# Activation tiles stored in pairs with 16 free bytes behind each pair

## The chip, the cores and the metric

The kernel runs on one core of a Trainium2 chip. The metric is the time on the device in microseconds (us); the kernel before takes 2249.84 us, the median of three runs (2249.45 to 2250.53).

## What is computed

Two layers of a decoder trunk on a sequence of 256 tokens, model width 2048. Cut to what matters:

```
for l in range(2):
    h = rms_norm(x, pre_mix_norm[l])
    p = h @ w_in[l]                      # 2048 x 5648: q, k, v, z, xBC, dt
    A = causal attention (8 heads x 128, rotary on 32 dims)
    S = Mamba-2 scan (16 heads x 64, 2 groups, state 128, chunks of 128)
    y = concat(rms_norm(A), group_rms_norm(S * silu(z))) @ w_out[l]     # 2048 x 2048
    x = x + rms_norm(y, post_mix_norm[l])
    u = square(relu(rms_norm(x, pre_mlp_norm[l]) @ w_up[l]))            # 2048 x 8192
    x = x + rms_norm(u @ w_down[l], post_mlp_norm[l])                   # 8192 x 2048
```

All inputs and outputs are float32.

## The kernel before

**Split products.** The large products are done in fp32r, TensorE's fast float32 form. To keep accuracy each operand is split in a high part and a rest: a product a * w becomes a_hi * w_hi + a_lo * w_hi + a_hi * w_lo, three matmuls. The order of these differs by line, their number doesn't.

**The weights' ring.** Weights come in chunks of 256 rows by 512 columns (NC = 8 chunks make a block of 2048 rows by 512 columns). SyncE's queue loads chunk c into raw[c % 4] (L296), ScalarE copies it to w_hi[c % 4] in fp32r (round_hi, L462), VectorE subtracts to get w_lo[c % 4] (split_lo, L1028), and TensorE then uses the chunk. ScalarE writes a slot once TensorE is done with it, SyncE's next load waits for split_lo. The ring has four slots, and the splitting runs three chunks ahead.

**The activations.** a_hi and a_lo hold the normed x, transposed: 16 tiles (k) of 128 partitions (features) by 256 tokens. u_hi and u_lo hold, at different times, the mixer's output and a quarter of the MLP's inner activations in the same form. Chunk c needs tiles 2c and 2c + 1, a pair. They are written by ScalarE (x_hi, L494; to_hi, L518; the square in up_pair, L646) and VectorE (x_lo, L1074; to_lo, L1089; L1375). In the mixer the first two pairs of u are also scratch of the scan, seg_hi and seg_lo, written by GpSimd (L416) and read by L825 and L826.

**Feature chunks and token chunks.** feature_chunk (L706) has the weights' tile as TensorE's stationary operand (128 x 128) and streams 256 columns of a: 24 matmuls of 256 columns per chunk (L734, 736, 737; for the first chunk after a norm L720, 722, 727). token_chunk (L690) has it the other way round: a 128 x 128 piece of a or u is stationary and 512 columns of w_hi or w_lo are streamed: 12 matmuls of 512 columns per chunk (L699 to 701). Feature chunks serve 7 of the 15 blocks of the mixer and the 16 blocks of w_up, token chunks the 8 other blocks of the mixer (v, z, w_out) and the 16 blocks of w_down, in each layer. inv_row_and_dt (L755) multiplies wdt_both, weights that lie outside the ring, with all 16 tiles of a (L769, 770).

**Order.** TensorE's program is written out by hand: block after block, chunk after chunk, with the small matmuls of attention and scan put in after chosen chunks. The MLP's four quarters run in a hardware loop, so that u's tiles are addressed there by a register (bass.ds).

**Where things lie.** Each tensor is a stretch of bytes in every partition; they lie one behind another in the order of their declaration (raw, w_hi, w_lo, x_sb, a_hi, a_lo, u_hi, u_lo, ybuf, xbcT, x_tok, v_tok, zg, b_tok, convr, wk, cbm, wdt_both, ident, ...), each rounded up to 32 bytes. raw to u_lo take 16,384 bytes each. A tile of a or u is 1024 bytes, a ring slot 4096.

Of the kernel before, what the change touches and what calls it, by code (L numbers as in the profile page):

```python
# [50 lines left out]
CK = 2  # L51
CB = 512
NC = KT // CK
W = CK * CB
WARM = 12
AHEAD = 3
# [70 lines left out]
def trunk(nc, x, positions, pre_mix_norm, post_mix_norm, pre_mlp_norm, post_mlp_norm, w_in, conv_w,  # L127
          conv_b, dt_bias, a_log, d_skip, attn_out_norm, ssd_out_norm, w_out, w_up, w_down, out):
    ctx = ExitStack()
    with ctx:  # L130
# [5 lines left out]
        w_hi = sb("w_hi", [P, RING, W], F32R)  # L136
        w_lo = sb("w_lo", [P, RING, W], F32R)
        x_sb = sb("x_sb", [P, TT, D])
        a_hi = sb("a_hi", [P, KT, SEQ], F32R)
        a_lo = sb("a_lo", [P, KT, SEQ], F32R)  # L140
        u_hi = sb("u_hi", [P, KT, SEQ], F32R)
        u_lo = sb("u_lo", [P, KT, SEQ], F32R)
        ybuf = sb("ybuf", [P, TT * D])
        xbcT = sb("xbcT", [P, NCT, SEQ])
        x_tok = sb("x_tok", [P, TT, SW])
# [50 lines left out]
        tab = x_tok[0:ROPE, :, :].rearrange("p t n -> p (t n)")  # L196
        tab_f, tab_m = tab[:, 0:HALF], tab[:, HALF:ROPE]
        tab_pos, tab_angle, tab_turn, tab_sin = (tab[:, i * SEQ:(i + 1) * SEQ] for i in range(1, 5))
        seg_hi = [u_hi[:, 2 * i:2 * i + 2].rearrange("p k s -> p (k s)") for i in range(2)]
        seg_lo = [u_lo[:, 2 * i:2 * i + 2].rearrange("p k s -> p (k s)") for i in range(2)]  # L200
        seg_e = wk[:, 1]
        tab_first, tab_last = x_tok[0:ROPE, 1, 2 * CB - 4:2 * CB], x_tok[0:ROPE, 1, 2 * CB - 8:2 * CB - 4]
        low_w, cmask_w, wdt_w = v_tok[:, 0, 0:P], v_tok[:, 0, P:2 * P], v_tok[:, 0, 2 * P:3 * P - 2 * SH]
# [243 lines left out]
        def _(act):  # L447
# [27 lines left out]
            with act.Fori(0, DEPTH) as l:  # L475
# [13 lines left out]
                def x_hi(n, j, gain):  # L489

                    act.wait_ge(*upto("xT_mm", l, 8 * n + j + 1))
                    for kk in range(2):
                        k = 2 * j + kk
                        ins = act.activation(a_hi[:, k], M[j % 4][:, kk * SEQ:(kk + 1) * SEQ], ACT.Copy,  # L494
                                             scale=prm[:, gain + k:gain + k + 1])
                    ins.then_inc(sem["xT_hi"], 1)

# [15 lines left out]
                def to_hi(name, n, j, bank, gain):  # L513

                    act.wait_ge(*upto(name + "_mm", l, n))
                    for kk in range(2):
                        k = 2 * j + kk
                        ins = act.activation(u_hi[:, k], M[bank][:, kk * SEQ:(kk + 1) * SEQ], ACT.Copy,  # L518
                                             scale=prm[:, gain + k:gain + k + 1])
                    ins.then_inc(sem[name + "_hi"], 1)  # L520

# [99 lines left out]
                def up_pair(q, i):  # L621

                    for j in range(2):
                        b = l * NB + q * (2 * QB) + i * 2 + (B_MLP + j)
                        first = j == 0 and is_first(q, i)
                        for c in range(AHEAD, NC + AHEAD):
                            split = (lambda: round_hi(b, c)) if c < NC else (lambda: round_hi(b + 1, c - NC))
                            if first:
                                norm_turn(1, c, G_MLP, split)
                            else:  # L630
                                split()
                        if first:
# [45 lines left out]
        def _(pe):  # L678
# [11 lines left out]
            def token_chunk(c, par, s_hi, s_lo, tile_first=False):  # L690


                for i in range(CK * TT):
                    kk, t = (i % CK, i // CK) if tile_first else (i // TT, i % TT)
                    k = c * CK + kk
                    wh, wl = (w[:, c % RING, kk * CB:(kk + 1) * CB] for w in (w_hi, w_lo))
                    o = acc[par][t][:]
                    sh, sl = (s[:, k, t * P:(t + 1) * P] for s in (s_hi, s_lo))
                    pe.matmul(o, sh, wh, start=(k == 0), stop=False)  # L699
                    pe.matmul(o, sh, wl, start=False, stop=False)  # L700
                    ins = pe.matmul(o, sl, wh, start=False, stop=(k == KT - 1))  # L701
                    if tile_first and i == CK - 1:
                        ins.then_inc(sem["tile_done"], 1)
                ins.then_inc(sem["mm_done"], 1)

            def feature_chunk(c, par, lo_ready=None):  # L706
# [8 lines left out]
                if lo_ready:  # L715

                    for kk in range(CK):
                        k = c * CK + kk
                        for m in range(CB // P):
                            pe.matmul(o(m), w(w_hi, kk, m), a_hi[:, k], start=(k == 0 and m % 2 == 0), stop=False,  # L720
                                      skip_group_check=True)
                            pe.matmul(o(m), w(w_lo, kk, m), a_hi[:, k], start=False, stop=False,
                                      skip_group_check=True)
                    pe.wait_ge(*lo_ready)
                    for kk in range(CK):
                        for m in range(CB // P):
                            ins = pe.matmul(o(m), w(w_hi, kk, m), a_lo[:, c * CK + kk], start=False, stop=False,
                                            skip_group_check=True)
                    ins.then_inc(sem["mm_done"], 1)
                    return  # L730
                for kk in range(CK):
                    k = c * CK + kk
                    for m in range(CB // P):
                        pe.matmul(o(m), w(w_hi, kk, m), a_hi[:, k], start=(k == 0 and m % 2 == 0), stop=False,  # L734
                                  skip_group_check=True)
                        pe.matmul(o(m), w(w_hi, kk, m), a_lo[:, k], start=False, stop=False, skip_group_check=True)  # L736
                        ins = pe.matmul(o(m), w(w_lo, kk, m), a_hi[:, k], start=False, stop=(k == KT - 1),  # L737
                                        skip_group_check=True)
                ins.then_inc(sem["mm_done"], 1)

            with pe.Fori(0, DEPTH) as l:
# [13 lines left out]
                def inv_row_and_dt():  # L755
# [259 lines left out]
        def _(dve):  # L1015
# [45 lines left out]
            with dve.Fori(0, DEPTH) as l:  # L1061
# [8 lines left out]
                def x_lo(n, j, gain):  # L1070
                    dve.wait_ge(*upto("xT_hi", l, 8 * n + j + 1))
                    for kk in range(2):
                        k = 2 * j + kk
                        ins = dve.scalar_tensor_tensor(a_lo[:, k], M[j % 4][:, kk * SEQ:(kk + 1) * SEQ],  # L1074
                                                       prm[:, gain + k:gain + k + 1], a_hi[:, k].bitcast(F32),
                                                       ALU.mult, ALU.subtract)
                    ins.then_inc(sem["xT_ready"], 1)

# [6 lines left out]
                def to_lo(name, n, j, bank, gain):  # L1085
                    dve.wait_ge(*upto(name + "_hi", l, n))
                    for kk in range(2):
                        k = 2 * j + kk
                        ins = dve.scalar_tensor_tensor(u_lo[:, k], M[bank][:, kk * SEQ:(kk + 1) * SEQ],  # L1089
                                                       prm[:, gain + k:gain + k + 1], u_hi[:, k].bitcast(F32),  # L1090
                                                       ALU.mult, ALU.subtract)
                    ins.then_inc(sem[name + "_ready"], 1)

# [248 lines left out]
                def up_pair(q, i):  # L1342
                    for j in range(2):
# [21 lines left out]
                        for k in range(2):  # L1365
# [9 lines left out]
                            dve.tensor_tensor(ul.rearrange("p k s -> p (k s)"), wk[:, 2 + k],  # L1375
                                              uh.rearrange("p k s -> p (k s)").bitcast(F32),
                                              ALU.subtract).then_inc(sem["u_ready"], 1)

                def down_pair(q, i):
                    for j in range(2):  # L1380
# [62 lines left out]
```

## Time and profile before

| | |
|---|---|
| median of three runs | 2249.84 us |
| span of the profiled execution (first to last instruction) | 2248.1 us |
| PE (TensorE matmuls) busy | 2216.5 us, 99% |
| DVE (VectorE) busy | 1319.9 us, 59% |
| ACT (ScalarE) busy | 1016.3 us, 45% |
| POOL (GpSimd) busy | 109.9 us, 5% |
| mean granted TensorE clock | 0.998 of full |
| HBM | 402.58 MB read, 180 GB/s over the span |

The profiled execution's own time is its span, 2248.1 us, 1.7 us under the median of the runs. Matmuls are pipelined: the record of one begins when it begins and ends when its last result is modelled to be out, while the next has long begun. So the busy time of PE counts overlapping records once, and the mean length of one says less than the distance from one start to the next, which the timeline gives.

### The profile page before, as it was taken

To read this page: it belongs to the slowest core of one execution; us is meant where nothing else is said; L and a number is where in the kernel's file an instruction comes from. 1 tells how busy PE (TensorE), PEld (TensorE's weight loads), DVE (VectorE), ACT (ScalarE), POOL (GpSimd) and SP (SyncE) were. 2 spreads that over 40 slices of the span, in tenths; PEclk is the share of its full clock that TensorE was granted. 3 is DMA by queue.
4 is the path that set the end of the run, shared out by engine and by line. 5 is a ranking of instruction groups with operands and counts; after the bars stand their busy time and mean duration, and the time that the engine had idled before them with its cause. 6 is when DMAs were issued, how large, how long until landed. Compare 5 with 4: busy or idle time off the path is not lost.

```text
span 2248.1 us, 39497 instructions
## 1 busy us (share of the span) xinstructions
PE 2216.5 (99%) x14282; PEld 2023.7 (90%) x14282; DVE 1319.9 (59%) x1528; ACT 1016.3 (45%) x1280; POOL 109.9 (5%) x112
## 2 busy tenths in 40 slices
PE   8999999999999999999999999999999999999997
PEld 8999888998998998898899988889989989988986
DVE  6777465655555455555578775657554545554555
ACT  5443464543444344344454435545434434443443
POOL 2141000000000000000001410000000000000000
PEclk9999999999999999999999999999999999999999
DMA  6555556556656656655645555655666566556565
GB/s 204 152 170 157 161 188 198 177 179 200 189 180 192 190 179 193 190 184 187 193 125 166 166 161 151 198 185 182 190 192 186 173 201 188 184 189 193 176 194 163
DMA packets 208448, 406.21 MB, mean 181 GB/s; under 512 B 12540, under 2 KB 12820, under 8 KB 207828
## 3 DMA queue, kind: packets, MB, share of 16 engines
q1 hardware_dynamic: 206660, 398.04, 57.3%
q10 hardware_dynamic: 992, 4.78, 0.6%
q0 software_dynamic: 688, 1.90, 0.4%
q8 instruction: 72, 1.18, 0.2%
q14 instruction: 36, 0.29, 0.0%
HBM read 402.58 MB, written 2.10 MB: 180 GB/s over the span
## 4 chain that ended last, share of the span: by engine, by line
issue 71%; PE 26%; DVE 1%; ACT 0%; POOL 0%; DMA 0%; DVEq 0%; POOLq 0%; ACTq 0%
PE acc L734 5%; PE acc L737 5%; PE acc L736 5%; PE acc L699 3%; PE acc L701 3%; PE acc L700 3%; PE M L838 1%; PE M L751 1%; DVE x_sb L1111 0%; PE M L859 0%; DVE xbcT L1177 0%; DMA wk<-in_ssd_out_norm 0%; PE M L879 0%; POOL st L393 0%; DVE w_lo L1028 0%
## 5 line engine op out<-in xcount | busy, mean ns | idle before, releaser
L1028 DVE TENSOR_TENSOR w_lo<-raw,w_hi 128x1024 fp32r<-128x1024 f32 x755 | 927.7, 1235 | 793.4 <-ACT w_hi L462 790.1
L462 ACT ACTIVATE w_hi<-raw 128x1024 fp32r<-128x1024 f32 x755 | 794.5, 1058 | 1026.8 <-PE acc L701 521.6
L734 PE MATMUL acc<-a_hi,w_hi 128*128 128x256 f32 x2912 | 828.4, 284 | 1.8 <-DVE w_lo L1028 1.8
L736 PE MATMUL acc<-a_lo,w_hi 128*128 128x256 f32 x2912 | 823.9, 283 | 0.0
L737 PE MATMUL acc<-a_hi,w_lo 128*128 128x256 f32 x2912 | 823.9, 283 | 0.0
L734 PEld LDWEIGHTS acc<-a_hi,w_hi 128*128 128x128 f32 x2912 | 558.6, 192 | 4.1 <-DVE w_lo L1028 2.7
L736 PEld LDWEIGHTS acc<-a_lo,w_hi 128*128 128x128 f32 x2912 | 558.7, 192 | 1.8 <-issue 1.0
L737 PEld LDWEIGHTS acc<-a_hi,w_lo 128*128 128x128 f32 x2912 | 558.7, 192 | 0.0
L699 PE MATMUL acc<-w_hi,u_hi 128*128 128x512 f32 x1280 | 498.6, 390 | 0.0
L700 PE MATMUL acc<-w_lo,u_hi 128*128 128x512 f32 x1280 | 498.0, 389 | 0.0
L701 PE MATMUL acc<-w_hi,u_lo 128*128 128x512 f32 x1280 | 498.0, 389 | 0.0
L701 PEld LDWEIGHTS acc<-w_hi,u_lo 128*128 128x128 f32 x1280 | 240.3, 188 | 50.0
L699 PEld LDWEIGHTS acc<-w_hi,u_hi 128*128 128x128 f32 x1280 | 240.3, 188 | 49.4
L700 PEld LDWEIGHTS acc<-w_lo,u_hi 128*128 128x128 f32 x1280 | 240.3, 188 | 49.4
L699 PE MATMUL acc<-w_hi,a_hi 128*128 128x512 f32 x256 | 102.6, 401 | 0.0
L701 PE MATMUL acc<-w_hi,a_lo 128*128 128x512 f32 x256 | 100.0, 391 | 0.0
L700 PE MATMUL acc<-w_lo,a_hi 128*128 128x512 f32 x256 | 99.8, 390 | 0.0
L393 POOL TENSOR_TENSOR st<-st,minus_half 128x2 f32<-128x2 f32 x12 | 9.1, 757 | 1786.3 <-DVE st L1100 1403.0
L1368 DVE TENSOR_TENSOR wk<-wk 128x512 f32<-128x512 f32 x64 | 44.0, 688 | 39.1 <-ACT wk L642 39.1
L642 ACT ACTIVATE wk<-acc 128x512 f32<-128x512 f32 x64 | 37.7, 589 | 62.2 <-PE acc L737 62.2
L701 PEld LDWEIGHTS acc<-w_hi,a_lo 128*128 128x128 f32 x256 | 48.0, 188 | 10.3
L700 PEld LDWEIGHTS acc<-w_lo,a_hi 128*128 128x128 f32 x256 | 48.2, 188 | 9.0
(218 smaller groups left out, 1049.2 us busy)
## 6 DMA issues: line engine op xcount, KB each, us to landing
raw<-in_w_up SPq DMA_DIRECT2D x256, 512.0 KB, 3.7
raw<-in_w_down SPq DMA_DIRECT2D x256, 512.0 KB, 4.5
raw<-in_w_in SPq DMA_DIRECT2D x179, 512.0 KB, 3.8
raw<-in_w_out SPq DMA_DIRECT2D x64, 512.0 KB, 4.6
zg<-in_post_mix_norm ACTq DMA_DIRECT2D x2, 1024.0 KB, 4.6
zg<-in_post_mlp_norm ACTq DMA_DIRECT2D x2, 1024.0 KB, 6.4
out<-x_sb SPq DMA_DIRECT2D x8, 256.0 KB, 2.8
x_sb<-in_x POOLq DMA_DIRECT2D x3, 512.0 KB, 7.3
```

The costliest lines, as they stand in the source:

```text
L462: act.activation(w_hi[:, c % RING], raw[:, c % RING], ACT.Copy).then_inc(sem["hi_ready"], 1)
L642: act.activation(wk[:, k], acc[1 - j][k][:], ACT.Relu).then_inc(acc_free[1 - j], 1)
L699: pe.matmul(o, sh, wh, start=(k == 0), stop=False)
L700: pe.matmul(o, sh, wl, start=False, stop=False)
L701: ins = pe.matmul(o, sl, wh, start=False, stop=(k == KT - 1))
L734: pe.matmul(o(m), w(w_hi, kk, m), a_hi[:, k], start=(k == 0 and m % 2 == 0), stop=False, skip_group_check=True)
L736: pe.matmul(o(m), w(w_hi, kk, m), a_lo[:, k], start=False, stop=False, skip_group_check=True)
L737: ins = pe.matmul(o(m), w(w_lo, kk, m), a_hi[:, k], start=False, stop=(k == KT - 1), skip_group_check=True)
L751: ins = pe.transpose(M[j % 4][:, kk * SEQ + t * P:kk * SEQ + (t + 1) * P], x_sb[:, t, k * P:(k + 1) * P], ident[:])
L838: ins = pe.matmul(M[3 * g][:, o:o + SP_], seg_e[:, h * P:(h + 1) * P], x_tok[:, t, g * CB + o:g * CB + o + SP_], start=True, stop=True)
L1028: dve.tensor_tensor(w_lo[:, c % RING], raw[:, c % RING], w_hi[:, c % RING].bitcast(F32), ALU.subtract).then_inc(sem["split_done"], 1)
L1368: dve.tensor_tensor(wk[:, 2 + k], wk[:, k], wk[:, k], ALU.mult)\
```

## The change

The four activation tensors get the shape [128, 8, 2 * 256 + 4] in place of [128, 16, 256]: each pair of tiles (2 KB) is followed by four float32 values, 16 bytes, that nothing writes or reads. A helper tile(a, k) gives tile k. All users of a_hi, a_lo, u_hi and u_lo address through it or through the pair; nothing else is changed.

```diff
+STEP = 4
-        a_hi = sb("a_hi", [P, KT, SEQ], F32R)
+        a_hi = sb("a_hi", [P, NC, CK * SEQ + STEP], F32R)
...
-        u_lo = sb("u_lo", [P, KT, SEQ], F32R)
+        u_lo = sb("u_lo", [P, NC, CK * SEQ + STEP], F32R)
...
-        seg_hi = [u_hi[:, 2 * i:2 * i + 2].rearrange("p k s -> p (k s)") for i in range(2)]
+        seg_hi = [u_hi[:, i, 0:2 * SEQ] for i in range(2)]
...
+        def tile(a, k):
+
+            return a[:, k // CK, k % CK * SEQ:(k % CK + 1) * SEQ]
...
-                            u = u_hi[:, 8 * i + 4 * j + 2 * k:8 * i + 4 * j + 2 * k + 2] if type(i) is int else \
-                                u_hi[:, bass.ds(i * 8 + (4 * j + 2 * k), 2)]
-                            act.activation(u.rearrange("p k s -> p (k s)"), wk[:, k], ACT.Square)\
+                            u = u_hi[:, 4 * i + 2 * j + k, 0:2 * SEQ] if type(i) is int else \
+                                u_hi[:, bass.ds(i * 4 + (2 * j + k), 1), 0:2 * SEQ].rearrange("p a n -> p (a n)")
+                            act.activation(u, wk[:, k], ACT.Square)\
...
-                    sh, sl = (s[:, k, t * P:(t + 1) * P] for s in (s_hi, s_lo))
+                    sh, sl = (tile(s, k)[:, t * P:(t + 1) * P] for s in (s_hi, s_lo))
...
-                        pe.matmul(o(m), w(w_hi, kk, m), a_lo[:, k], start=False, stop=False, skip_group_check=True)
-                        ins = pe.matmul(o(m), w(w_lo, kk, m), a_hi[:, k], start=False, stop=(k == KT - 1),
+                        pe.matmul(o(m), w(w_hi, kk, m), tile(a_lo, k), start=False, stop=False, skip_group_check=True)
+                        ins = pe.matmul(o(m), w(w_lo, kk, m), tile(a_hi, k), start=False, stop=(k == KT - 1),
...
-                        pe.matmul(o, w, a_hi[:, k], start=(k == 0), stop=False)
-                        ins = pe.matmul(o, w, a_lo[:, k], start=False, stop=(k == KT - 1))
+                        pe.matmul(o, w, tile(a_hi, k), start=(k == 0), stop=False)
+                        ins = pe.matmul(o, w, tile(a_lo, k), start=False, stop=(k == KT - 1))
...
-                            k0 = i * 8 + (4 * j + 2 * k)
-                            uh, ul = (a[:, k0:k0 + 2] if type(i) is int else a[:, bass.ds(k0, 2)]
+                            k0 = i * 4 + (2 * j + k)
+                            uh, ul = (a[:, k0, 0:2 * SEQ] if type(i) is int else
+                                      a[:, bass.ds(k0, 1), 0:2 * SEQ].rearrange("p a n -> p (a n)")
```

x_hi, to_hi, x_lo, to_lo and the first chunk's matmuls (L720, 722, 727) change in the same way, a[:, k] to tile(a, k).

## Rows read from the trace of the kernel before

**Rows 1.** The page: span, and PE's busy time, its share and instructions.
```profile
span 2248.1 us, 39497 instructions
...
PE 2216.5 (99%) x14282; PEld 2023.7 (90%) x14282; DVE 1319.9 (59%) x1528; ACT 1016.3 (45%) x1280; POOL 109.9 (5%) x112
```

**Rows 2.** The page: the chain that ended last, by engine.
```profile
issue 71%; PE 26%; DVE 1%; ACT 0%; POOL 0%; DMA 0%; DVEq 0%; POOLq 0%; ACTq 0%
```

**Rows 3.** Waits of PE: line, waited for: us in total, times, longest.
```profile
PE M L683 <- DMA wk<-in_ssd_out_norm: 8.7, 1, 8.7
```

**Rows 4.** Groups by line, PE: out<-in, shapes, count | busy us, mean ns.
```profile
L734 PE MATMUL acc<-a_hi,w_hi 128*128 128x256 f32 x2912 | 828.4, 284 | 1.8 <-DVE w_lo L1028 1.8
...
L699 PE MATMUL acc<-w_hi,u_hi 128*128 128x512 f32 x1280 | 498.6, 390 | 0.0
...
L699 PE MATMUL acc<-w_hi,a_hi 128*128 128x512 f32 x256 | 102.6, 401 | 0.0
```

**Rows 5.** Timeline, feature chunk, first and last of 18: start us, length us, instruction.
```profile
799.90 0.28 PE L734 MATMUL acc<-a_hi,w_hi 128*128 128x256 f32 x1
...
801.94 0.28 PE L737 MATMUL acc<-a_hi,w_lo 128*128 128x256 f32 x1
```

**Rows 6.** Timeline, token chunks, first and last of 22.
```profile
900.02 0.39 PE L701 MATMUL acc<-w_hi,u_lo 128*128 128x512 f32 x1
...
904.78 0.39 PE L701 MATMUL acc<-w_hi,u_lo 128*128 128x512 f32 x1
```

**Rows 7.** Timeline, dt projection: of 5 early ones, then of 25 later ones.
```profile
41.64 0.28 PE L770 MATMUL M<-a_lo,wdt_both 128*128 128x256 f32 x1
...
42.12 0.28 PE L770 MATMUL M<-a_lo,wdt_both 128*128 128x256 f32 x1
...
42.34 0.28 PE L770 MATMUL M<-a_lo,wdt_both 128*128 128x256 f32 x1
...
45.06 0.28 PE L770 MATMUL M<-a_lo,wdt_both 128*128 128x256 f32 x1
```

**Rows 8.** Timeline, fp32 matmuls: ident with itself; probabilities with values, six pairs.
```profile
396.68 2.84 PE L926 MATMUL M<-ident 128*128 128x128 f32 x24
...
1399.67 0.38 PE L892 MATMUL M<-v_tok,wk 128*128 128x128 f32 x2
...
1400.79 0.39 PE L895 MATMUL M<-v_tok,wk 128*128 128x128 f32 x2
```

**Rows 9.** Timeline, token chunk just after small matmuls, first and last of 5.
```profile
1391.73 0.40 PE L700 MATMUL acc<-w_lo,a_hi 128*128 128x512 f32 x1
...
1392.65 0.39 PE L701 MATMUL acc<-w_hi,a_lo 128*128 128x512 f32 x1
```

**Rows 10.** Groups by line, DVE and ACT: the writes of u.
```profile
L1375 DVE TENSOR_TENSOR u_lo<-wk,u_hi 128x512 f32 (+1 forms) x64 | 44.3, 692 | 13.7 <-ACT u_hi L646 7.0 <-DVE wk L1368 5.7
...
L646 ACT ACTIVATE u_hi<-wk 128x512 f32 (+1 forms) x64 | 40.5, 633 | 7.1
```

**Rows 11.** Waits of ACT for PE.
```profile
ACT w_hi L462 <- PE acc L701: 521.6, 332, 2.3
ACT w_hi L462 <- PE acc L737: 496.9, 280, 5.2
```

**Rows 12.** Timeline, DVE and ACT beside a feature chunk.
```profile
801.91 1.22 DVE L1028 TENSOR_TENSOR w_lo<-raw,w_hi 128x1024 fp32r<-128x1024 f32 x1 [1.66 <-ACT w_hi L462]
803.70 1.06 ACT L462 ACTIVATE w_hi<-raw 128x1024 fp32r<-128x1024 f32 x1 [1.82 <-PE acc L737]
```

**Rows 13.** Windows, mixer and MLP of layer 1: busy us by engine, PEclk, DMA share, GB/s.
```profile
26.00:412.00 386.00, 382.59 (x2472) 346.84 (x2471) 259.17 (x351) 182.08 (x266) 47.98 (x34) 1.00 0.55 166
412.00:1134.00 722.00, 718.49 (x4620) 657.63 (x4619) 391.48 (x388) 316.50 (x357) 2.71 (x4) 1.00 0.60 187
```

**Rows 14.** The page: loads of w_down, count, KB, us from issue to landing.
```profile
raw<-in_w_down SPq DMA_DIRECT2D x256, 512.0 KB, 4.5
```

More of the change, by code:

```diff
@@ L138, in trunk @@
         x_sb = sb("x_sb", [P, TT, D])
-        a_hi = sb("a_hi", [P, KT, SEQ], F32R)
-        a_lo = sb("a_lo", [P, KT, SEQ], F32R)
-        u_hi = sb("u_hi", [P, KT, SEQ], F32R)
-        u_lo = sb("u_lo", [P, KT, SEQ], F32R)
+        a_hi = sb("a_hi", [P, NC, CK * SEQ + STEP], F32R)
+        a_lo = sb("a_lo", [P, NC, CK * SEQ + STEP], F32R)
+        u_hi = sb("u_hi", [P, NC, CK * SEQ + STEP], F32R)
+        u_lo = sb("u_lo", [P, NC, CK * SEQ + STEP], F32R)
         ybuf = sb("ybuf", [P, TT * D])
@@ L198, in trunk @@
         tab_pos, tab_angle, tab_turn, tab_sin = (tab[:, i * SEQ:(i + 1) * SEQ] for i in range(1, 5))
-        seg_hi = [u_hi[:, 2 * i:2 * i + 2].rearrange("p k s -> p (k s)") for i in range(2)]
-        seg_lo = [u_lo[:, 2 * i:2 * i + 2].rearrange("p k s -> p (k s)") for i in range(2)]
+        seg_hi = [u_hi[:, i, 0:2 * SEQ] for i in range(2)]
+        seg_lo = [u_lo[:, i, 0:2 * SEQ] for i in range(2)]
         seg_e = wk[:, 1]
@@ L493, in x_hi @@
                         k = 2 * j + kk
-                        ins = act.activation(a_hi[:, k], M[j % 4][:, kk * SEQ:(kk + 1) * SEQ], ACT.Copy,
+                        ins = act.activation(tile(a_hi, k), M[j % 4][:, kk * SEQ:(kk + 1) * SEQ], ACT.Copy,
                                              scale=prm[:, gain + k:gain + k + 1])
@@ L517, in to_hi @@
                         k = 2 * j + kk
-                        ins = act.activation(u_hi[:, k], M[bank][:, kk * SEQ:(kk + 1) * SEQ], ACT.Copy,
+                        ins = act.activation(tile(u_hi, k), M[bank][:, kk * SEQ:(kk + 1) * SEQ], ACT.Copy,
                                              scale=prm[:, gain + k:gain + k + 1])
@@ L719, in feature_chunk @@
                         for m in range(CB // P):
-                            pe.matmul(o(m), w(w_hi, kk, m), a_hi[:, k], start=(k == 0 and m % 2 == 0), stop=False,
+                            pe.matmul(o(m), w(w_hi, kk, m), tile(a_hi, k), start=(k == 0 and m % 2 == 0), stop=False,
                                       skip_group_check=True)
-                            pe.matmul(o(m), w(w_lo, kk, m), a_hi[:, k], start=False, stop=False,
+                            pe.matmul(o(m), w(w_lo, kk, m), tile(a_hi, k), start=False, stop=False,
                                       skip_group_check=True)
@@ L726, in feature_chunk @@
                         for m in range(CB // P):
-                            ins = pe.matmul(o(m), w(w_hi, kk, m), a_lo[:, c * CK + kk], start=False, stop=False,
+                            ins = pe.matmul(o(m), w(w_hi, kk, m), tile(a_lo, c * CK + kk), start=False, stop=False,
                                             skip_group_check=True)
@@ L733, in feature_chunk @@
                     for m in range(CB // P):
-                        pe.matmul(o(m), w(w_hi, kk, m), a_hi[:, k], start=(k == 0 and m % 2 == 0), stop=False,
+                        pe.matmul(o(m), w(w_hi, kk, m), tile(a_hi, k), start=(k == 0 and m % 2 == 0), stop=False,
                                   skip_group_check=True)
-                        pe.matmul(o(m), w(w_hi, kk, m), a_lo[:, k], start=False, stop=False, skip_group_check=True)
-                        ins = pe.matmul(o(m), w(w_lo, kk, m), a_hi[:, k], start=False, stop=(k == KT - 1),
+                        pe.matmul(o(m), w(w_hi, kk, m), tile(a_lo, k), start=False, stop=False, skip_group_check=True)
+                        ins = pe.matmul(o(m), w(w_lo, kk, m), tile(a_hi, k), start=False, stop=(k == KT - 1),
                                         skip_group_check=True)
@@ L1073, in x_lo @@
                         k = 2 * j + kk
-                        ins = dve.scalar_tensor_tensor(a_lo[:, k], M[j % 4][:, kk * SEQ:(kk + 1) * SEQ],
-                                                       prm[:, gain + k:gain + k + 1], a_hi[:, k].bitcast(F32),
+                        ins = dve.scalar_tensor_tensor(tile(a_lo, k), M[j % 4][:, kk * SEQ:(kk + 1) * SEQ],
+                                                       prm[:, gain + k:gain + k + 1], tile(a_hi, k).bitcast(F32),
                                                        ALU.mult, ALU.subtract)
@@ L1088, in to_lo @@
                         k = 2 * j + kk
-                        ins = dve.scalar_tensor_tensor(u_lo[:, k], M[bank][:, kk * SEQ:(kk + 1) * SEQ],
-                                                       prm[:, gain + k:gain + k + 1], u_hi[:, k].bitcast(F32),
+                        ins = dve.scalar_tensor_tensor(tile(u_lo, k), M[bank][:, kk * SEQ:(kk + 1) * SEQ],
+                                                       prm[:, gain + k:gain + k + 1], tile(u_hi, k).bitcast(F32),
                                                        ALU.mult, ALU.subtract)
@@ L1371, in up_pair @@
                             dve.wait_ge(*upto("u_hi_ready", l, n + 1))
-                            k0 = i * 8 + (4 * j + 2 * k)
-                            uh, ul = (a[:, k0:k0 + 2] if type(i) is int else a[:, bass.ds(k0, 2)]
+                            k0 = i * 4 + (2 * j + k)
+                            uh, ul = (a[:, k0, 0:2 * SEQ] if type(i) is int else
+                                      a[:, bass.ds(k0, 1), 0:2 * SEQ].rearrange("p a n -> p (a n)")
                                       for a in (u_hi, u_lo))
-                            dve.tensor_tensor(ul.rearrange("p k s -> p (k s)"), wk[:, 2 + k],
-                                              uh.rearrange("p k s -> p (k s)").bitcast(F32),
-                                              ALU.subtract).then_inc(sem["u_ready"], 1)
+                            dve.tensor_tensor(ul, wk[:, 2 + k], uh.bitcast(F32), ALU.subtract)\
+                                .then_inc(sem["u_ready"], 1)
                 def down_pair(q, i):
```

## The prediction

> **What bounds the kernel now.** I read the engine shares first: PE is busy for 2216.5 of 2248.1 us [rows 1]. "Busy" overlaps here, so I then read the chain of waits: 71% of the span is "issue", time in which the instruction at the end of the chain waited for nothing that the profile shows, and 26% is PE itself [rows 2]. PE's longest wait for another engine is 8.7 us, once, before the first matmul [rows 3]. So the end is set by how closely one matmul follows another. The groups by line show what these matmuls are [rows 4]: feature matmuls with 256 moving columns (L734, 736, 737, 2912 of each) and token matmuls with 512 (L699 to 701, 1536 of each over the two kinds of input, of which the rows show 1280 and 256). With the 96 of L720, 722 and 727 that makes 8832 + 4608 = 13,440 split-precision matmuls. The 283 and 390 ns in these rows are the time of one from start to modelled end; what counts is from start to start. In the timeline 17 feature steps take 801.94 - 799.90 = 2.04 us, 120.0 ns each [rows 5]; 21 token steps take 904.78 - 900.02 = 4.76 us, 226.7 ns each [rows 6]. 8832 x 120.0 + 4608 x 226.7 ns = 1060 + 1045 = 2105 us of the span of 2248.1: nothing else is large.
>
> At the granted full clock (2.4 GHz, PEclk 1.00 in the windows [rows 13]) 256 columns are 106.7 ns and 512 are 213.3 ns. Each matmul thus costs 13.3 ns more than its columns, the same for both lengths. It is a price for each matmul and its weight load, not for each column. That price is what the change can touch.
>
> **Is the price tied to addresses?** Tensors lie one behind another in the order in which they are declared. In w_hi, w_lo, a_hi, a_lo, u_hi and u_lo every tile that a main matmul reads starts at a multiple of 512 bytes from the others, so the weights being loaded and the operand being streamed always stand at distance 0 modulo 128 bytes. One group of the same form doesn't: the dt projection (L769, 770) takes its weights from wdt_both, behind convr, whose 4144 bytes are rounded up to 4160, so they stand 64 bytes off modulo 128. Its 256-column matmuls begin at the usual pace (41.64 to 42.12 us, four steps, 120 ns), and then settle: 24 steps take 45.06 - 42.34 = 2.72 us, 113.3 ns each [rows 7]. The difference of 6.67 ns is 16 columns at 2.4 GHz, and 13.3 ns is twice that. 120.0, 226.7 and 113.3 ns are 18, 34 and 17 such steps: the pace looks quantized, and an operand's place seems to decide whether one quantum is lost or two. Against it: fp32 matmuls don't care. With ident as both operands (distance 0) 24 take 2.84 us, (2.84 - 0.275) / 23 = 111.5 ns; with wk and v_tok, 64 bytes apart modulo 128, 10 steps take 1400.79 - 1399.67 = 1.12 us, 112 ns [rows 8]. Those stream each column in two passes, so they are weaker evidence than the dt group, but dt also differs from the rest by lying far away in SBUF.
>
> A rule of the Trainium skill speaks against the change here. The page "SBUF — State Buffer", section "Who interferes with whom", gives PE separate read ports for the moving operand and for the weights, and says that PE and ACT never wait on anyone; by it the sum would be zero. The traces agree only for the fp32 rows; the 6.67 ns of the dt rows has no place in it. The page "TensorE: Matmul & The Clock Gate", section "Back-to-back issue gap", would put a warm matmul of 256 columns at 109.2 ns; that this kernel's stands at 120.0 is a price that the page doesn't have.
>
> **The change part by part.** (1) Pair p of a and u starts at p x 2064 bytes instead of p x 2048, and each of the four tensors grows by 128 bytes. Modulo 128 the tensors' bases, and all that is behind them, stay where they were, and pair p is 16p bytes off: 0, 16, ..., 112. Chunk c of every block reads pair c with ring slot c % 4, so one eighth of all main matmuls (1680) meets each distance. Chunk 0 is unchanged. (2) One quantum saved in an eighth is 1680 x 6.67 ns = 11.2 us, feature and token alike, since the price is per matmul (that it also holds for token matmuls, where u or a is the weight, is not shown by any row). (3) How many of the seven shifted eighths gain? The trace shows distance 64 alone (pair 4). Ends: one eighth, 11.2 us; all seven, 78.4 us. Below nothing: a distance could also lose a quantum; seven that lose one are +78.4 us. The nearest row for a slower pace is the token matmuls after a pause, 1392.65 - 1391.73 = 0.92 us for four, 230 ns [rows 9], only half a quantum. I take four eighths, as if the loss faded evenly from distance 0 to 64 and back (weights 0, 1/4, 1/2, 3/4, 1, 3/4, 1/2, 1/4 sum to 4): 4 x 11.2 = 44.8 us. (4) The dt matmuls are 64, and pairs 0 and 4 change roles there: below 0.5 us. The segment-sum weights on POOL and L825, 826 keep pairs 0 and 1: 32 matmuls, nothing.
>
> (5) The instructions keep their number and shapes: tile() gives the same 256 contiguous values, the u writes remain 512 contiguous values, and the register index is i * 4 instead of i * 8. ACT and DVE write 64 such tiles each, 633 and 692 ns a piece [rows 10]; were they a tenth slower it would be 4.0 and 4.4 us of their time, hidden because ACT waits 1018.5 us for PE in all [rows 11]. With that cover gone it would cost those 4 us. The weights' DMAs don't change.
>
> (6) What is late next, once PE is faster? A chunk of 24 feature matmuls takes 2.88 us; ACT and DVE spend 1.06 and 1.22 us on it [rows 12], and both finish long before the slot is used again. DVE is busy for 259 of 386 us in the mixer and 391 of 722 in the MLP [rows 13]. A raw slot is freed at 801.91 + 1.22 = 803.13 us and wanted by ACT at 803.70 - 2.88 + 4 x 2.88 = 812.3 us: 9.2 us for a load that lands in 4.5 us [rows 14]. The DMA rate rises from 187 to about 191 GB/s at a share of 0.60. So I let nothing come back.
>
> Sum: against the profiled execution's 2248.1 us, 2248.1 - 44.8 = 2203.3 us. The median of the runs is 1.7 us above that span: 2205.0 us.
>
> **Rivals.** No change: the 13.3 ns are PE's own price for a fp32r weight swap whatever the address, and dt is faster for another reason (its weights' region, or always writing one place in PSUM). For: the pace is 120 for every m, k and ring slot, and the fp32 rows. Against: within the feature matmuls, too, the written half bank stays for three matmuls and none of these is at 113. Time 2249.8 us. Slower: at some distances the weight load runs just behind the stream over the same lines and catches it more often, a third quantum. It decides as soon as more eighths lose than gain; with five up and two down it is net three, +33.6 us, 2283 us. For: distance 0 may be a favourable meeting, as the ident rows, at 111.5 ns the fastest non-transposing ones here, have it; against: dt at 64 is faster, and no steady pace in this trace is above 226.7 or 120.0. Gain eaten: PE speeds up but the mixer, where DVE is busiest, makes PE wait for split chunks; half is given back, 2227 us; the slack in (6) speaks against it.
>
> **How the numbers follow.** PE's pace improves for one to seven eighths: 0.48, with its own range 2171 (2249.8 - 78.4) to 2239 (2249.8 - 11.2). No change: 0.29. Slower: 0.18. Gain eaten: 0.05, also faster. Differences below 0.2% (4.5 us) can't be told from none here. Faster is 0.48 + 0.05 = 0.53, same 0.29, slower 0.18. The range holds the first two cases and the fourth, and some of the third: 2170 to 2258; the rest of slower, about 0.15, is left out.
>
> **What would show it.** In the changed kernel the start-to-start time, chunk by chunk, is the whole test: chunk 0 still at 120.0 and 226.7 ns, chunk 4 at 113.3 and 220.0, the other six at one or the other. The dt group should invert: pair 4 at 120. PE's other waits stay within a few us, and ACT's wait for PE shrinks by about the gain. If all eight chunks stay at 120.0 the address idea is wrong; if chunk 4 alone gains, the time is 2239; if token chunks don't follow feature chunks, step (2) is wrong, and the eighths are worth 7.4 us each.

## The result and the profile after

The changed kernel is slower: 2258.98 us (median of 5 runs, 2258.76 to 2259.58) against 2249.82 us for the kernel before (5 runs, 2249.32 to 2250.53). The ratio is 1.0042, with a 95% interval of 1.003 to 1.0055: small, but clear of the noise.

The page of the changed kernel, span and busy times, answers to [rows 1]:

```profile
span 2257.7 us, 39497 instructions
...
PE 2226.5 (99%) x14282; PEld 2010.4 (89%) x14282; DVE 1319.0 (58%) x1528; ACT 1016.8 (45%) x1280; POOL 111.7 (5%) x112
...
issue 71%; PE 26%; DVE 1%; ACT 0%; POOL 0%; DMA 0%; DVEq 0%; POOLq 0%; ACTq 0%
```

Instructions, chain and the busy times of the other engines are those of before; PE alone has 10.0 us more. Its waits for others hardly grew (for w_lo from 1.8 to 2.2 us in all); the first row answers to [rows 3] (8.7 us):

```profile
PE M L688 <- DMA wk<-in_ssd_out_norm: 8.6, 1, 8.6
PE M L756 <- DVE x_sb L1116: 4.1, 3, 2.2
```

So the matmuls themselves came at another pace. The groups by line show that it went both ways. They answer to [rows 4], where L734 (now L739) had 284 ns, L699 (now L704) 390 ns with u and 401 with a:

```profile
L739 PE MATMUL acc<-a_hi,w_hi 128*128 128x256 f32 x2912 | 820.0, 282 | 2.2 <-DVE w_lo L1033 2.2
L742 PE MATMUL acc<-a_hi,w_lo 128*128 128x256 f32 x2912 | 818.6, 281 | 0.0
L741 PE MATMUL acc<-a_lo,w_hi 128*128 128x256 f32 x2912 | 815.7, 280 | 0.0
...
L704 PE MATMUL acc<-w_hi,u_hi 128*128 128x512 f32 x1280 | 506.6, 396 | 0.0
...
L704 PE MATMUL acc<-w_hi,a_hi 128*128 128x512 f32 x256 | 103.8, 405 | 0.0
```

Feature matmuls became shorter by 1 to 3 ns, token matmuls longer by 4 to 6. The timeline gives the pace. First a block of feature chunks: the first matmul of its chunk 0 and of its chunk 7, 168 steps later.

```profile
811.74 0.28 PE L739 MATMUL acc<-a_hi,w_hi 128*128 128x256 f32 x1
...
831.55 0.28 PE L739 MATMUL acc<-a_hi,w_hi 128*128 128x256 f32 x1
```

19.81 / 168 = 117.9 ns, where [rows 5] had 120.0. Then a block of token chunks, 84 steps:

```profile
677.11 0.40 PE L704 MATMUL acc<-w_hi,u_hi 128*128 128x512 f32 x1
...
696.59 0.39 PE L704 MATMUL acc<-w_hi,u_hi 128*128 128x512 f32 x1
```

19.48 / 84 = 231.9 ns, where [rows 6] had 226.7. Nor is the pace even any more. These are seven steps within a chunk 4:

```profile
823.06 0.28 PE L739 MATMUL acc<-a_hi,w_hi 128*128 128x256 f32 x1
823.17 0.28 PE L741 MATMUL acc<-a_lo,w_hi 128*128 128x256 f32 x1
823.29 0.28 PE L742 MATMUL acc<-a_hi,w_lo 128*128 128x256 f32 x1
823.41 0.28 PE L739 MATMUL acc<-a_hi,w_hi 128*128 128x256 f32 x1
...
823.76 0.28 PE L739 MATMUL acc<-a_hi,w_hi 128*128 128x256 f32 x1
823.88 0.28 PE L741 MATMUL acc<-a_lo,w_hi 128*128 128x256 f32 x1
```

Every three matmuls (w_hi with a_hi, w_hi with a_lo, w_lo with a_hi) take 0.35 us, but the single steps repeat as about 118, 114 and 122 ns. Before, all were 120.

From here on "pace" is the mean distance from one start to the next over all matmuls of a kind in a trace, steps over 140 ns (feature) and 245 ns (token) left out, which are pauses.

| | feature | token on a | token on u |
|---|---|---|---|
| matmuls | 8832 | 768 | 3840 |
| before, ns | 119.93 | 227.95 | 226.76 |
| changed, ns | 118.00 | 232.03 | 232.70 |
| difference x count, us | -17.0 | +3.1 | +22.8 |

The sum is +8.9 us, and 9.2 us were measured: all but 0.3 us of the result is the pace of PE.

By chunk, with the hi parts at 0, 16, ..., 112 bytes from the ring and the lo parts 128 bytes further, the changed kernel's feature pace is 117.87, 117.92, 117.79, 117.65, 117.72, 118.19, 118.17, 118.65 ns. The token pace (u, w_down) is 232.5, 234.9, 232.5, 231.3, 231.6, 232.6, 233.0, 232.9. Chunk 0, which I held to be unchanged, is as different as the rest, and no chunk stands at 113.3. The dt group, of which I had said that pair 4 would go to 120, slowed as a whole: its last 24 steps take 118.2 ns on average, where they took 113.3.

### The profile page after: what moved, and what is told of

Its sections match the earlier page's. It is cut to its first block, busy times and chain, and to the rows that moved or that the text cites. A ratio compares the mean times of both kernels' runs of the same rounds, so it can differ in the third digit from the quotient of the medians.

```text
span 2257.7 us, 39497 instructions
## 1 busy us (share of the span) xinstructions
PE 2226.5 (99%) x14282; PEld 2010.4 (89%) x14282; DVE 1319.0 (58%) x1528; ACT 1016.8 (45%) x1280; POOL 111.7 (5%) x112
## 4 chain that ended last, share of the span: by engine, by line
issue 71%; PE 26%; DVE 1%; ACT 0%; POOL 0%; DMA 0%; DVEq 0%; POOLq 0%; ACTq 0%
PE acc L739 5%; PE acc L742 5%; PE acc L741 4%; PE acc L704 3%; PE acc L706 3%; PE acc L705 3%; PE M L843 1%; PE M L756 1%; PE M L864 0%; DVE xbcT L1182 0%; DVE x_sb L1116 0%; DMA wk<-in_ssd_out_norm 0%; PE acc L725 0%; PE M L884 0%; POOL st L398 0%
## 5 line engine op out<-in xcount | busy, mean ns | idle before, releaser
L739 PE MATMUL acc<-a_hi,w_hi 128*128 128x256 f32 x2912 | 820.0, 282 | 2.2 <-DVE w_lo L1033 2.2
L741 PE MATMUL acc<-a_lo,w_hi 128*128 128x256 f32 x2912 | 815.7, 280 | 0.0
L739 PEld LDWEIGHTS acc<-a_hi,w_hi 128*128 128x128 f32 x2912 | 549.2, 189 | 4.6 <-DVE w_lo L1033 3.1
L741 PEld LDWEIGHTS acc<-a_lo,w_hi 128*128 128x128 f32 x2912 | 547.2, 188 | 1.9 <-issue 1.0
L742 PEld LDWEIGHTS acc<-a_hi,w_lo 128*128 128x128 f32 x2912 | 547.9, 188 | 0.0
L704 PE MATMUL acc<-w_hi,u_hi 128*128 128x512 f32 x1280 | 506.6, 396 | 0.0
L705 PE MATMUL acc<-w_lo,u_hi 128*128 128x512 f32 x1280 | 505.1, 395 | 0.0
L706 PE MATMUL acc<-w_hi,u_lo 128*128 128x512 f32 x1280 | 505.0, 395 | 0.0
L704 PEld LDWEIGHTS acc<-w_hi,u_hi 128*128 128x128 f32 x1280 | 240.6, 188 | 55.2
L704 PE MATMUL acc<-w_hi,a_hi 128*128 128x512 f32 x256 | 103.8, 405 | 0.0
```

Of the source, the lines that this page charges most:

```text
L739: pe.matmul(o(m), w(w_hi, kk, m), tile(a_hi, k), start=(k == 0 and m % 2 == 0), stop=False, skip_group_check=True)
L741: pe.matmul(o(m), w(w_hi, kk, m), tile(a_lo, k), start=False, stop=False, skip_group_check=True)
L742: ins = pe.matmul(o(m), w(w_lo, kk, m), tile(a_hi, k), start=False, stop=(k == KT - 1), skip_group_check=True)
```

## The experiments

The kernel before ran beside each of them, with medians of 2249.4 to 2249.6 us. The granted clock was 0.997 or 0.998 of full in all traces.

**Which part does it?** First the bases alone, 128 free bytes behind each tensor and no gaps inside:

```diff
         a_hi = sb("a_hi", [P, KT, SEQ], F32R)
+        tail0 = sb("tail0", [P, 32])
         a_lo = sb("a_lo", [P, KT, SEQ], F32R)
+        tail1 = sb("tail1", [P, 32])
...
```

> No gaps inside the tensors, but 128 free bytes behind each of a_hi, a_lo, u_hi and u_lo, so that their bases stand where the changed kernel has them. Base theory (the 128 bytes between a hi part and its lo part do it, as chunk 0 of the changed kernel, whose pair has no gap ahead of it, also left 120.0 ns): feature matmuls at about 117.9 ns, token matmuls at about 232.5 ns in every chunk, near 2259 us. Gap theory (the growing distance between ring and pair does it): 120.0 and 226.7 ns, 2250 us. The theory of the prediction, distance modulo 128: 2250 us.

Measured: 2251.13 us, ratio 1.0007 (0.9998 to 1.0017). Feature 117.79 ns, the same in all chunks; token on a 231.2, on u 231.12. One block of each, 168 feature steps and 84 token steps:

```profile
607.25 0.28 PE L738 MATMUL acc<-a_hi,w_hi 128*128 128x256 f32 x1
...
627.04 0.28 PE L738 MATMUL acc<-a_hi,w_hi 128*128 128x256 f32 x1
...
854.29 0.39 PE L703 MATMUL acc<-w_hi,u_hi 128*128 128x512 f32 x1
...
873.71 0.39 PE L703 MATMUL acc<-w_hi,u_hi 128*128 128x512 f32 x1
```

19.79 / 168 = 117.8 ns and 19.42 / 84 = 231.2 ns. Both paces moved, in opposite directions, and the shifts cancel in the total: by the total alone, nothing happened. A move by 128 bytes is not neutral, which ends the prediction's "modulo 128". The base theory was right in its direction, and about the feature pace. Its time, 2259 us, was missed by 8 us, because the token pace is 231.1 and not 232.5. So the two parts of the change divide like this: the moved bases give the whole gain of the feature matmuls and three quarters of the loss of the token matmuls, +1.7 us together, and the 16-byte gaps add the other 7.9 of the 9.2 us (1.6 ns more on each of the 3840 token matmuls that read u are 6.1 us of it).

Gaps in a alone (after's tile() kept, u without gaps and declared first):

```diff
+        u_hi = sb("u_hi", [P, NC, CK * SEQ], F32R)
+        u_lo = sb("u_lo", [P, NC, CK * SEQ], F32R)
         a_hi = sb("a_hi", [P, NC, CK * SEQ + STEP], F32R)
         a_lo = sb("a_lo", [P, NC, CK * SEQ + STEP], F32R)
-        u_hi = sb("u_hi", [P, NC, CK * SEQ + STEP], F32R)
-        u_lo = sb("u_lo", [P, NC, CK * SEQ + STEP], F32R)
```

> The 16-byte gaps in a_hi and a_lo alone; u_hi and u_lo are declared first, without gaps, at the old distances. Role theory (an operand off the ring's alignment speeds the matmuls in which it is streamed up, 119.9 to 118.0 ns, and slows those in which it is the stationary one, 227 to 232.6 ns): 8832 feature matmuls gain 17 us, the 768 token matmuls that read a lose 4 us, 2237 us. If gaps in any tensor slow the whole: over 2250 us. The prediction's theory has no loss in it, so it would want 2250 or less for this one too.

Measured: 2236.74 us, ratio 0.9943 (0.9927 to 0.996). By line, feature and token on u:

```profile
L739 PE MATMUL acc<-a_hi,w_hi 128*128 128x256 f32 x2912 | 819.8, 282 | 2.2 <-DVE w_lo L1033 2.2
...
L704 PE MATMUL acc<-w_hi,u_hi 128*128 128x512 f32 x1280 | 498.7, 390 | 0.0
```

Gaps in u alone (a_hi and a_lo without, u_hi and u_lo with them):

> The gaps in u_hi and u_lo alone. Role theory: feature matmuls stay at 119.9 ns, the 3840 token matmuls that read u lose 5.6 ns each, 2250 + 22 = 2272 us. If only gaps in the streamed operand mattered: 2250 us.

Measured: 2273.29 us, ratio 1.0105 (1.0088 to 1.0122). The same two lines:

```profile
L739 PE MATMUL acc<-a_hi,w_hi 128*128 128x256 f32 x2912 | 828.3, 284 | 1.8 <-DVE w_lo L1033 1.8
...
L704 PE MATMUL acc<-w_hi,u_hi 128*128 128x512 f32 x1280 | 506.6, 396 | 0.0
```

The two halves are separate and add up: -12.7 (a) and +23.9 (u) make +11.2 us, where both together measured 9.2. Only the matmuls that read the moved tensor change: token on u stays at 226.8 ns with gaps in a, feature at 119.9 with gaps in u. The role theory puts it so: moved a is a gain, since most matmuls on it stream it; moved u is a loss, since all matmuls on it hold it as the stationary operand while the ring is streamed. The role theory's times, 2237 and 2272 us, were met within 1.3 us.

All four tensors at a common 64 bytes, which is the dt projection's distance:

```diff
+        ahead = sb("ahead", [P, 16])
         a_hi = sb("a_hi", [P, KT, SEQ], F32R)
```

> No gaps, but 64 free bytes ahead of a_hi: all four tensors stand 64 bytes off the ring, their hi and lo parts at the old distance from each other. Distance theory of the prediction (64 bytes is the dt projection's distance, 113.3 ns): feature 113.3 and token 220.0 ns in every chunk, 13,440 x 6.67 ns less, 2160 us. If it holds for the streamed role only, and tokens lose 5.6 ns: 2250 - 59 + 26 = 2217 us. If a common distance does nothing and only unequal hi and lo parts do: 2250 us.

Measured: 2258.4 us, ratio 1.004 (1.0026 to 1.0054). Feature 117.50 ns, token 233.3 in every chunk; here 84 token steps of one block:

```profile
676.44 0.39 PE L700 MATMUL acc<-w_hi,u_hi 128*128 128x512 f32 x1
...
696.04 0.39 PE L700 MATMUL acc<-w_hi,u_hi 128*128 128x512 f32 x1
```

19.60 / 84 = 233.3 ns. A common distance with hi and lo in step changes both paces, so it is not only the distance between hi and lo that counts. But 64 bytes do not give a mean of 113.3 (2160 us; 24 of the 368 feature chunks have that pace), and the mixed forecast of 2217 us failed as well, because it took 113.3 for the feature matmuls.

**A map of distances.** Pair of hi, pair of lo and a gap in one tensor, so that hi and lo of a chunk always keep the same distance and chunk c stands at c gaps. The edit for gaps of 128 bytes (32 floats):

```diff
+        a_both = sb("a_both", [P, NC, 2 * CK * SEQ + 32], F32R)
+        a_hi, a_lo = (a_both[:, :, i * CK * SEQ:(i + 1) * CK * SEQ] for i in range(2))
```

> u_hi and u_lo at the old distances. a_hi and a_lo lie in one tensor, pair by pair (pair of hi, pair of lo, 128 free bytes), so that hi and lo of a chunk always stand at the same distance from the ring modulo 2048, and chunk c at 128c bytes: a scan of 0, 128, ..., 896 with equal parts. If only the distance between streamed parts mattered (the 128 bytes between a_hi and a_lo in the changed kernel), or if the distance counts modulo 128: feature 120.0 ns in all chunks, 2250 us. If the distance between weights and streamed operand counts in a longer period: 120.0 in chunk 0, about 117 to 118 in the others; the 768 token matmuls of a about 232 ns where a is off; some 2237 us.

> The same with 16 free bytes: chunk c at 16c bytes, hi and lo alike, a scan of 0 to 112. If any distance but 0 gives the pace of the run with all 64 off: feature 120.0 in chunk 0, about 117.5 in the seven others, 2249.4 - 7/8 x 8832 x 2.4 ns + token matmuls of a 768 x 7/8 x 6.3 ns = 2235 us. If a distance below 32 or 64 bytes still meets the same place: 120.0 in chunks 1 to 3 too, 2242 us.

> The 16-byte scan with 128 bytes ahead of it: chunk c at 128 + 16c bytes. If the period is 128 bytes: the same list as in the first scan (119.7, 118.7, 116.8, 118.3, 117.4, 119.8, 119.9, 113.8), 2237 us. If it is 256 bytes, as the 128-byte scan says (119.7 at even multiples, 118.9 at odd ones): 118.9 in chunk 0 and another list behind it; 2230 to 2245 us.

> The scan with 4 free bytes: chunk c at 4c bytes, 0 to 28. If SBUF is read in lines of 16 bytes and only the line counts: chunks 0 to 3 at one pace near 120.0 ns, chunks 4 to 7 near the 118.7 of 16 bytes. If an operand that starts within a line also costs a line more: chunks 1 to 3 and 5 to 7 slower than 0 and 4. If single bytes count: a different pace in each. Between 2235 and 2260 us.

Measured: 2246.5 us for the scan by 128 bytes (ratio 0.9987, 0.9978 to 0.9997), 2236.9 for 16 (0.9945, 0.9928 to 0.9961), 2237.94 for 16 with 128 ahead (0.9948, 0.9931 to 0.9964), and 2241.3 in one run for 4 bytes. Feature pace by chunk, ns:

| chunk | 0 | 1 | 2 | 3 | 4 | 5 | 6 | 7 |
|---|---|---|---|---|---|---|---|---|
| 128c bytes | 119.67 | 118.82 | 119.68 | 118.97 | 119.70 | 118.82 | 119.68 | 118.90 |
| 16c | 119.72 | 118.74 | 116.77 | 118.31 | 117.43 | 119.77 | 119.86 | 113.80 |
| 128 + 16c | 119.08 | 118.68 | 118.16 | 119.22 | 115.67 | 119.23 | 118.12 | 117.30 |
| 4c | 119.48 | 122.62 | 117.55 | 116.70 | 113.82 | 122.09 | 120.32 | 115.88 |

The first line alternates: the even multiples of 128 bytes are alike, and so are the odd ones, so the pattern repeats after 256 bytes. The second and third lines differ, as they may if 128 bytes are not the period. (They prove less than the first, because one distance can have more than one pace, as the last experiment shows.) The last line says that bytes count, down to 4: 122.6 at 4 bytes is the slowest pace of all, and my guess of 16-byte lines fell. All mean token paces on a in these scans are 228.4 ns or more: no distance beats 226.7.

The forecasts did less well than some of the times suggest. The 128-byte scan met neither of its two (2250 and 2237 us): the odd multiples came to 118.9 and not to 117 or 118, and the even ones stayed. The 16-byte scan's 2236.9 lies beside its 2235, but by luck: the chunks spread from 113.8 to 119.9 ns instead of standing at 117.5. The ranges for the other two held, and were wide.

**Is the dt projection fast because of its distance?**

```diff
+        pad0 = sb("pad0", [P, 16])
         w_lo = sb("w_lo", [P, RING, W], F32R)
+        pad1 = sb("pad1", [P, 240])
...
+        pad2 = sb("pad2", [P, 16])
         wdt_both = sb("wdt_both", [P, 2 * KT * SH + P - 2 * SH], F32R)
```

> a and u as in the kernel before, at distance 0 from w_hi (modulo 1024); w_lo 64 bytes further off, and wdt_both moved by 64 bytes, so that the dt projection now stands at distance 0 modulo 128. The prediction's reading of the dt rows: dt slows from 113.3 to 120.0 ns. Against it (its pace has another cause): dt stays near 113.3. For the main matmuls: w_lo is now off both as weights (feature) and as stream (token), so feature about 118 and token about 232 ns if every matmul next to an off one is touched, 2258 us; if nothing but a and u's own place matters, 2250 us.

Measured: 2254.39 us, ratio 1.0021 (1.0011 to 1.003). The last 23 matmuls of the dt projection, first and last:

```profile
42.34 0.27 PE L773 MATMUL M<-a_lo,wdt_both 128*128 128x256 f32 x1
...
44.92 0.28 PE L773 MATMUL M<-a_lo,wdt_both 128*128 128x256 f32 x1
```

2.58 / 22 = 117.3 ns against 113.3 in [rows 7]: it does depend on the addresses. It is no test of distance 0, though. With a period of 256 bytes, and since the dt weights step by 128 bytes from k to k, dt stood at 64 and 192 bytes in turn before, and stands at 0 and 128 in turn here.

Distance, or the place of one operand? The dt groups of three runs answer it. In the kernel before, a is at 0 and wdt_both at 64 or 192, modulo 256. In this run a is at 0 and wdt_both at 0 or 128. In the run with a alone at 64 bytes (below), wdt_both is at 0 or 128 as here, and a at 64. There the last 24 steps are:

```profile
41.51 0.28 PE L771 MATMUL M<-a_lo,wdt_both 128*128 128x256 f32 x1
...
44.23 0.28 PE L771 MATMUL M<-a_lo,wdt_both 128*128 128x256 f32 x1
```

2.72 / 24 = 113.3 ns, the pace of before. Both operands stand elsewhere than before, at the same distance, and the pace is the same; the weights stand as in this run, at another distance, and the pace is another. So it is the distance that counts for dt.

Moving w_lo alone, with a and u in place, changes the main matmuls too:

```profile
608.15 0.28 PE L737 MATMUL acc<-a_hi,w_hi 128*128 128x256 f32 x1
...
627.93 0.28 PE L737 MATMUL acc<-a_hi,w_hi 128*128 128x256 f32 x1
...
855.53 0.39 PE L702 MATMUL acc<-w_hi,u_hi 128*128 128x512 f32 x1
...
875.01 0.40 PE L702 MATMUL acc<-w_hi,u_hi 128*128 128x512 f32 x1
```

19.78 / 168 = 117.7 ns and 19.48 / 84 = 231.9 ns; the means over the kernel are 117.81 (feature) and 232.0 (token on u), as in the fork of 2258 us. The time was 2254.4, and the shifts in pace come to +4.4 us of the 4.9 measured: -18.7 for the feature matmuls, +23.1 for the token matmuls.

This also corrects the role theory. w_lo is the stationary operand of a feature matmul and the streamed one of a token matmul, the reverse of a and u, and still the feature matmuls gain and the token matmuls lose. So it doesn't matter which of the two operands is moved. What separates gain from loss is the kind of matmul: feature matmuls stream 256 columns, token matmuls 512, and their order of hi and lo differs. No run separates these, so why the two kinds answer in opposite ways stays open.

**A version that beats both.** First a at 64 bytes with u in place (64 free bytes ahead of a_hi), then a at 112, the distance of chunk 7 in the scan. The edit of the second:

```diff
+OFF = 28
...
-        a_hi = sb("a_hi", [P, KT, SEQ], F32R)
-        a_lo = sb("a_lo", [P, KT, SEQ], F32R)
         u_hi = sb("u_hi", [P, KT, SEQ], F32R)
         u_lo = sb("u_lo", [P, KT, SEQ], F32R)
+        a_both = sb("a_both", [P, OFF + 2 * KT * SEQ], F32R)
+        a_hi, a_lo = (a_both[:, OFF + i * KT * SEQ:OFF + (i + 1) * KT * SEQ].rearrange("p (k s) -> p k s", s=SEQ)
+                      for i in range(2))
```

> u at the old distance, a_hi and a_lo both 64 bytes off. Role theory: feature 117.5 ns as in the run with all 64 off, token matmuls of u 227 ns, of a 233.3 ns: 2249.4 - 8832 x 2.4 ns + 768 x 6.3 ns = 2233 us, below both kernels. If the whole of the program had to share one alignment: no better than 2258 us.

> u at the old distance, all of a_hi and a_lo 112 bytes off the ring. In the 16-byte scan chunk 7, at 112 bytes, ran at 113.8 ns, the others at 116.8 to 119.9. If the pace is a function of the distance alone: feature 113.5 ns in all chunks, token matmuls of a 232.7, 2249.5 - 8832 x 6.4 ns + 768 x 5 ns = 2197 us. If chunk 7's pace came from what stands before and behind it (chunk 6 at 96 bytes, chunk 0 at 0): about 118 ns, 2237 us.

Measured at 64 bytes: 2233.23 us, ratio 0.993 (0.9914 to 0.9947), feature 117.45, token on a 233.3, on u 226.8, as expected. Measured at 112 bytes: **2200.52 us, ratio 0.9782 (0.9766 to 0.9799)**, 49.1 us under the kernel before (the forecast was 2197; its premise, one pace for one distance, falls with the next experiment). Its page and 168 feature steps of one block:

```profile
span 2198.7 us, 39497 instructions
...
PE 2165.6 (98%) x14282; PEld 1968.2 (90%) x14282; DVE 1316.4 (60%) x1528; ACT 1017.6 (46%) x1280; POOL 115.5 (5%) x112
```

```profile
791.94 0.28 PE L736 MATMUL acc<-a_both,w_hi 128*128 128x256 f32 x1
...
810.98 0.28 PE L736 MATMUL acc<-a_both,w_hi 128*128 128x256 f32 x1
```

19.04 / 168 = 113.3 ns, in chunk after chunk. The mean over the kernel is 113.68: 8832 x 6.25 = 55.2 us less, the token matmuls on a 4 us more. The rest of the kernel follows a PE that is faster by 2.2% of the time: its waits for w_lo are 3.0 us in all where they were 1.8, and the others are those of before. After other matmuls PE does not have this pace at once:

```profile
147.22 0.28 PE L736 MATMUL acc<-a_both,w_hi 128*128 128x256 f32 x1
...
148.64 0.28 PE L736 MATMUL acc<-a_both,w_hi 128*128 128x256 f32 x1
...
149.66 0.28 PE L736 MATMUL acc<-a_both,w_hi 128*128 128x256 f32 x1
```

The first 12 steps take 1.42 / 12 = 118.3 ns each, the next 9 take 1.02 / 9 = 113.3, with nothing between them.

**One distance, more than one pace.** At 16 bytes the scans had shown 118.7 ns once and 113.8 once. So a at a common 16 bytes (OFF = 4):

> u at the old distance, all of a_hi and a_lo 16 bytes off the ring. At 16 bytes two paces have been seen: 118.7 ns in chunk 1 of the 16-byte scan, entered from distance 0, and 113.8 in chunk 4 of the 4-byte scan, entered from distance 12. If the pace were a function of the distance alone, only one of these could be; if PE falls into one of several rhythms depending on how it enters a chunk, then with one distance throughout it should keep one rhythm: either 113.3 ns in nearly all chunks and about 2200 us, or 118.7 and about 2243 us, or chunks of both kinds in different blocks, between.

Measured: 2239.15 us, ratio 0.9954 (0.9938 to 0.9971). Rows around a pause: 24 steps before it, the pause (L779, small transposes), 24 steps after it. (Feature matmuls run on from 50.40 us to the pause, and from the pause to 56.20 us.)

```profile
47.68 0.28 PE L736 MATMUL acc<-a_both,w_hi 128*128 128x256 f32 x1
...
50.40 0.28 PE L736 MATMUL acc<-a_both,w_hi 128*128 128x256 f32 x1
...
53.13 0.38 PE L779 MATMUL M<-ident,wk 128*128 128x128 f32 x2
...
56.20 0.28 PE L736 MATMUL acc<-a_both,w_hi 128*128 128x256 f32 x1
...
59.05 0.28 PE L736 MATMUL acc<-a_both,w_hi 128*128 128x256 f32 x1
```

2.72 / 24 = 113.3 ns before and 2.85 / 24 = 118.8 after, on operands at the same distances. 116.5 and 116.9 ns are found too. The pace changes 26 times from one feature chunk to the next in this trace: 24 times other matmuls stand between the two, twice PE waited for 1.3 us, and never does it change without a break. In the MLP, where nothing interrupts the blocks, all chunks but the first after a norm stay at 118.7. The token matmuls of the 16-byte scan show the same in chunk 1 of two blocks, nine steps each time:

```profile
230.42 0.39 PE L706 MATMUL acc<-w_hi,a_both 128*128 128x512 f32 x1
...
232.46 0.39 PE L706 MATMUL acc<-w_hi,a_both 128*128 128x512 f32 x1
...
258.43 0.40 PE L706 MATMUL acc<-w_hi,a_both 128*128 128x512 f32 x1
...
260.53 0.39 PE L706 MATMUL acc<-w_hi,a_both 128*128 128x512 f32 x1
```

2.04 / 9 = 226.7 ns, and 2.10 / 9 = 233.3. So the last of the three forecasts came true, chunks of both kinds. The run with a at 64 bytes has two feature paces as well:

```profile
94.10 0.28 PE L735 MATMUL acc<-a_hi,w_hi 128*128 128x256 f32 x1
...
99.54 0.28 PE L735 MATMUL acc<-a_hi,w_hi 128*128 128x256 f32 x1
...
425.52 0.28 PE L735 MATMUL acc<-a_hi,w_hi 128*128 128x256 f32 x1
...
439.66 0.28 PE L735 MATMUL acc<-a_hi,w_hi 128*128 128x256 f32 x1
```

5.44 / 48 = 113.3 ns and 14.14 / 120 = 117.8: 28 of its 368 feature chunks, nearly all in the mixer, keep the first, the others the second, and its mean of 117.45 is a mixture. The pace is a rhythm into which PE falls. The paces found differ from distance to distance, and at 16 and 64 bytes PE went from one to another only where other matmuls or a wait stood between. What makes the rhythm inside PE wasn't shown. So the numbers in the table of distances, where each chunk is entered from another distance, need not be the only paces that these distances can have.

## Why the prediction was wrong

It said 2205 us (2170 to 2258), faster; it came out at 2258.98, slower, by 9.2 us. The step that failed is (2), which gave token matmuls the gain of feature matmuls.

- *What bounds the kernel*: right. PE's start-to-start times are the whole of the time, and their differences explain 8.9 of 9.2 us. That ACT, DVE and the loads would not matter (steps 5 and 6) was right as well: even the kernel that takes 2.2% less time has only 1.2 us more of waits for w_lo.
- *The price of 13.3 ns belongs to addresses*: right as far as it goes. It is 6.67 ns at 112 bytes in the feature matmuls, so at least half of it hangs on addresses; the other half stood in every run. The rival "no change" is refuted.
- *Step 2 failed, "one quantum saved in an eighth is worth the same, feature and token alike"*. This decides the sign. The reading was drawn from dt, where a is streamed, and carried over to the 4608 token matmuls by a sentence that admitted that no row showed it. There the pace of 226.7 is the best one found, and every move made the mean longer: by 4.4 to 6.6 ns for the matmuls on u, by 3.1 to 5.4 for those on a. In the changed kernel it is +25.9 us where about -15 had been in the sum. The prediction's own sign for this, "if token chunks don't follow feature chunks, step (2) is wrong", is what the trace shows.
- *Step 3's term was mis-sized*: 4 eighths of a quantum were to bring the feature matmuls to 116.7 ns, -29 us; they came to 118.0, -17.0 us. Its shape was wrong too: no eighth stands at 120 or at 113.3, and the paces form a list without order, not a slope to 64 bytes.
- *Step 1, "modulo 128 the bases stay where they were", failed*: with bases moved by 128 bytes and no gaps, feature fell to 117.8 and token rose to 231.1. The period is 256 bytes, so even chunk 0 was changed: a_lo stands 128 bytes off in it, and so does u_lo.
- *The inference from the dt rows* was half right: distance matters, and for dt it is the distance itself (113.3 ns at the same distance with both operands moved, 117.3 at another). But dt's 113.3 was not the pace of 64 bytes. With the ring 64 bytes off, 28 of 368 feature chunks have 113.3 and the others 117.8. dt stands at 64 and 192 bytes in turn, takes each weight tile twice and steps by 128 bytes from k to k, where the ring's tiles step by 512. Which of these keeps dt at 113.3 wasn't tried.
- *The rival that ended slower* had the right sign, by luck: its place was wrong. It had some distances slower in all matmuls; what came is all chunks slower in one kind of matmul, and faster in the other.
- The Trainium skill's page "TensorE: Matmul & The Clock Gate", section "Step-by-step: what each phase is for", says that loading the next weights doesn't steal read bandwidth from the running matmul. In this case's fp32r matmuls the two are not independent: moving only w_lo by 64 bytes changes the feature pace from 119.9 to 117.8 ns and the token pace from 226.8 to 232.0, and dt keeps its 113.3 ns when both operands move together. Whether what they share is read bandwidth wasn't shown.

## What to carry to other kernels

When PE is busy all the time and each fp32r matmul costs more than its columns, look at the starts in the timeline: a pace that stays constant and lies above the time of the columns (here 120.0 against 106.7 ns) may be a rhythm that a few bytes in an operand's address change. Keep the kinds of matmul apart in such a sum, and measure each by itself: here 112 bytes in front of the tensor that the feature matmuls read are worth 2.2%, and 16-byte gaps in the one that token matmuls alone read cost 1%. A pace taken from one group of matmuls is that of its pattern of addresses and of what ran before it, not of one distance. A total that doesn't move can be two shifts that cancel.

## What the runs showed of the hardware that I had not expected

- The pace of fp32r matmuls depends on the distance between the operand streamed and the weights loaded: 113.3 to about 123 ns for 256 columns, 226.7 to about 235 for 512, repeating after 256 bytes in the 128-byte scan, and with differences between steps of 4 bytes.
- Steady paces can be cycles of unequal steps, as 118, 114, 122 ns above.
- At one distance, 16 bytes, PE kept 113.3, 116.5, 116.9 or 118.7 ns, and changed from one to another only after a pause or after other matmuls. At 112 bytes it went from 118.3 to 113.3 within a chunk, with no break.
